# Last eight modulation chunks moved from the first feed-forward stage into the latent inverse, with columns by transposes and one fill copy placed earlier

## What is computed

```
mod   = silu(c)     @ w_mod + b_mod          # w_mod: 1024 x 6144, fp32, 24 MB
mod_c = silu(c_ctx) @ w_mod + b_mod
sh1, sc1, g1, sh2, sc2, g2 = split(mod, 6)   # shifts, scales and gates, 1024 values each
h  = rmsnorm(x) * norm1_g * (1 + sc1) + sh1            # latent
hc = rmsnorm(ctx) * norm1_g * (1 + csc1) + csh1        # context
... delta rule on hc, then on h; each needs the inverse of a unit lower triangular matrix per head and chunk
x = x + g1 * mix
x = x + g2 * swiglu(rmsnorm(x) * norm2_g * (1 + sc2) + sh2)
```

## Time and profile before

| | us |
|---|---|
| median of 3 runs (lowest, highest) | 1394.09 (1393.87, 1400.3) |
| the profiled execution's own time | 1391.02 |
| its span in the trace | 1389.0 |
| busy: PE / DVE / ACT / POOL | 1302.8 / 819.8 / 641.0 / 124.6 |

### The profile page before, as it was taken

How to read it: one execution, slowest core, us unless ns; L and a number is a source line. 1 busy time by engine, 2 the same in 40 slices (tenths; PEclk the granted TensorE clock), 3 DMA queues, 4 the chain that set the end, 5 groups by cost and what they waited for, 6 DMA issues and landing times.

```text
span 1389.0 us, 22276 instructions
## 1 busy us (share of the span) xinstructions
PE 1302.8 (94%) x9222; PEld 1189.4 (86%) x9222; DVE 819.8 (59%) x1189; ACT 641.0 (46%) x950; POOL 124.6 (9%) x108
## 2 busy tenths in 40 slices
PE   7987999999999999789999989988889999999997
PEld 6964988888898889679999988988789998899996
DVE  6672464544685756676655586576644566654444
ACT  6353353443556635434444356454136453544443
POOL 0130000000002112140001030023310000000000
PEclk9997999999999999999999999999999999999999
DMA  9558467776554344234443444542004555355540
GB/s 320 164 189 267 141 221 242 242 245 227 178 181 152 92 138 136 91 122 152 152 152 123 159 145 122 152 122 92 30 1 135 183 173 179 130 189 190 190 151 31
DMA packets 163802, 218.74 MB, mean 157 GB/s; under 512 B 5016, under 2 KB 134902, under 8 KB 163574
## 3 DMA queue, kind: packets, MB, share of 16 engines
q1 hardware_dynamic: 161842, 215.15, 47.5%
q10 hardware_dynamic: 1860, 2.16, 0.5%
HBM read 216.26 MB, written 1.05 MB: 156 GB/s over the span
## 4 chain that ended last, share of the span: by engine, by line
PE 64%; issue 20%; DVE 6%; ACT 2%; POOL 2%; DMA 2%; DVEq 2%; POOLq 2%; ACTq 0%; SPq 0%
PE bank L539 17%; PE bank L540 17%; PE bank L541 17%; PE bank L602 2%; DVE w_lo L530 1%; PE bank L1317 1%; DMA w_raw<-in_w_mod 1%; PE bank L1295 1%; PE bank L1524 1%; PE bank L824 1%; PE bank L1377 1%; PE bank L812 1%; PE bank L1302 1%; DVEq L2171 1%; DMA arena<-in_vec_rows 1%
## 5 line engine op out<-in xcount | busy, mean ns | idle before, releaser
L530 DVE TENSOR_TENSOR w_lo<-w_raw,w_hi 128x1024 fp32r<-128x1024 f32 (+1 forms) x350 | 423.4, 1250 | 167.8 <-ACT w_hi L521 161.5
L539 PE MATMUL bank<-act_hi,w_hi 128*128 128x256 f32 x1744 | 505.0, 290 | 18.2 <-DVE act_lo L2139 5.1
L540 PE MATMUL bank<-act_lo,w_hi 128*128 128x256 f32 x1744 | 498.5, 286 | 0.0
L541 PE MATMUL bank<-act_hi,w_lo 128*128 128x256 f32 x1744 | 498.1, 286 | 0.0
L521 ACT ACTIVATE w_hi<-w_raw 128x1024 fp32r<-128x1024 f32 (+1 forms) x350 | 348.9, 1041 | 102.8 <-PE bank L541 89.9
L539 PEld LDWEIGHTS bank<-act_hi,w_hi 128*128 128x128 f32 x1744 | 339.7, 195 | 33.7 <-issue 19.4
L540 PEld LDWEIGHTS bank<-act_lo,w_hi 128*128 128x128 f32 x1744 | 339.9, 195 | 1.0 <-issue 0.5
L541 PEld LDWEIGHTS bank<-act_hi,w_lo 128*128 128x128 f32 x1744 | 339.5, 195 | 0.0
L539 PE MATMUL bank<-w_hi,side_hi 128*128 128x512 f32 (+1 forms) x392 | 151.1, 386 | 0.0
L540 PE MATMUL bank<-w_lo,side_hi 128*128 128x512 f32 (+1 forms) x392 | 148.6, 379 | 0.0
L541 PE MATMUL bank<-w_hi,side_lo 128*128 128x512 f32 (+1 forms) x392 | 148.4, 379 | 0.0
(11 more groups left out here) (323 smaller groups left out, 1540.8 us busy)
## 6 DMA issues: line engine op xcount, KB each, us to landing
w_raw<-in_w_in SPq DMA_DIRECT2D x40, 1024.0 KB, 5.8
w_raw<-in_w_up SPq DMA_DIRECT2D x32, 1024.0 KB, 6.4
w_raw<-in_w_down SPq DMA_DIRECT2D x32, 1024.0 KB, 5.0
w_raw<-in_w_mod SPq DMA_DIRECT2D x24, 1024.0 KB, 5.3
w_raw<-in_w_ffn_in SPq DMA_DIRECT2D x22, 1024.0 KB, 5.2
w_raw<-in_w_gate SPq DMA_DIRECT2D x20, 1024.0 KB, 5.3
w_raw<-in_w_ffn_out SPq DMA_DIRECT2D x11, 1024.0 KB, 5.3
w_raw<-in_w_out SPq DMA_DIRECT2D x8, 1024.0 KB, 8.0
```

The lines of the kernel that those rows point to most:

```text
L530: nc.vector.tensor_tensor(wlo[:, slot, 0:n], raw[:, st.slot(name), n * half:n * (half + 1)], whi[:, slot, 0:n].bitcast(F32), ALU.subtract) ...
L539: nc.tensor.matmul(o, ahi, bhi, start=start, stop=False, skip_group_check=True)
L540: nc.tensor.matmul(o, ahi, blo, start=False, stop=False, skip_group_check=True)
L541: return nc.tensor.matmul(o, alo, bhi, start=False, stop=stop, skip_group_check=True)
```

## The change

1. `LATE_MODS = 8`: only pairs 6 and 7 stay in layer 0's feed-forward. Chunks 16 to 23 (pairs 8 to 11) are put in the stream behind the chunk `("post", 16)`, the first one of the branch merge, and are multiplied in the latent delta at points of the inverse.
2. The columns of every pair (also of 0 to 7) are made by four transposes of 128x128 against the identity; DVE sums the four strips with a reduce out of PSUM and adds the bias in a second instruction. The matrix `mod_sum` is gone.
3. `final_g` is computed with pair 3 (not with the last pair), the gains of the second norm with pair 9.
4. `settle()`: ACT copies `sc3`'s bank right before it copies the turned k and v, ahead of the chunk loop, and not at T0.
5. The rows of pairs 8 to 11 are copied into two scratch tiles of the delta (`scr[0]`, `scr[1]`).

```diff
+LATE_MODS = 8
-        ... ("pad", 1), ("mod_sum", 2),
+        ... ("pad", 1),
-    put("mod_sum", p % 32 == np.arange(2)[None, :])
+LAT_EXTRA = {"P": [("mod", 16), ("mod", 17), ("modr", 8)], "x0": [("modc", 8), ("mod", 18), ("mod", 19), ("modr", 9)],
+             "x1": [("modc", 9)], "z2": [("mod", 20)], "x2": [("mod", 21), ("modr", 10)], "t2": [("modc", 10)],
+             "z3": [("mod", 22)], "x3": [("mod", 23), ("modr", 11)], "t3": [("modc", 11)]}
+LAST_FILL = 6 + len(LAT_FILL)
-def filler(part, step):
+def filler(part, step, between=None):
...
     def fill(point, most=None):
+        for entry in LAT_EXTRA.get(point, []) if between else []:
+            between(*entry)
-for j in range(6, MOD_PAIRS):
+for j in range(6, LATE_MODS):
     for at, entry in ((0, ("mod", 2 * j)), (2, ("mod", 2 * j + 1)), (3, ("modr", j)), (4, ("modc", j))):
         FFN_EXTRA[0].setdefault(16 + 4 * (j - 6) + at, []).append(entry)
+LAT_MODS = mod(*range(2 * LATE_MODS, 2 * MOD_PAIRS))
...
         for l, src in enumerate(post_src):
             st.add(("post", l), src)
+            if l == LAST_FILL:
+                add_direct(LAT_MODS)
...
             act.drain().then_inc(S("dn_ecol"), 1)
+            if settle:
+                settle()
             for n in range(TT):
...
+        def rows_of(j):
+            return mod_rows[j % 4] if j < LATE_MODS else scr[j % 2]
...
                 for i in range(4):
-                    mm = nc.tensor.matmul(ps[b][:, 2 * i:2 * i + 2], mod_rows[j % 4][:, P * i:P * (i + 1)],
-                                          col("mod_sum", 0, 2), start=True, stop=True)
+                    mm = tr(ps[b][:, P * i:P * (i + 1)], rows_of(j)[:, P * i:P * (i + 1)])
...
+            def lat_mod(kind, x):          # PE; ACT's takes "modr", DVE's takes "modc"
+                if kind == "mod":
+                    mod_chunk(x, take)
+                elif kind == "modc":
+                    mod_columns(x)
...
-                if i:
+                if i and i - 1 not in settled:
                     lat_copy(i - 1)
+            def settle():
+                lat_copy(left[0] - 1)
+                settled.append(left[0] - 1)
...
-                free(v.tensor_tensor(modc[:, 4 * j:4 * j + 4, :], ps[b][:, 0:8].rearrange("p (m j) -> p m j", j=2),
-                                     bm, ALU.add), b)
+                parts = ps[b][:, :].rearrange("p (m k j) -> p m j k", m=4, k=4)[:, :, 0:2, :]
+                free(v.tensor_reduce(modc[:, 4 * j:4 * j + 4, :], parts, AX.X, ALU.add), b)
+                dve.drain()
+                v.tensor_tensor(modc[:, 4 * j:4 * j + 4, :], modc[:, 4 * j:4 * j + 4, :], bm, ALU.add)
...
-                if j == MOD_PAIRS - 1:
+                if j == 9:
                     dve.drain()
                     gain_of(2, "norm2_g_2", 32, 0)
+                if j == 3:
                     fn = vec[:, V["final_norm"]:V["final_norm"] + KT]
                     ...                    # final_g, as before
```

More of the change, by code:

```diff
@@ L70, in const_columns @@
     for name, width in (
-        ("ident", P), ("ones", P), ("rot", P), ("eps", 1), ("ln_q", 1), ("eps2", 1), ("even", 1), ("inv_freq", 1), ("pad", 1), ("mod_sum", 2),
+        ("ident", P), ("ones", P), ("rot", P), ("eps", 1), ("ln_q", 1), ("eps2", 1), ("even", 1), ("inv_freq", 1), ("pad", 1),
         ("mask", 3 * 384), ("inv_cnt", 2 * T),
@@ L908, in act_lat_inputs, with act_delta @@
             ln_exp_tables()
-        def act_delta(act, part, d_, fill):
+        def act_delta(act, part, d_, fill, settle=None):
             lat = part == "lat"
@@ L1545, in lat_fill @@
                 project(pe, ("post", n_tiles + i), lambda m: (b, T * m), KT, all_hi, all_lo)
+            def lat_mod(kind, x):
[3 more added lines that the diff above has]
+                    mod_columns(x)
             pe_lat_inputs(pe, take)
-            pe_delta(pe, "lat", D_LAT, take, filler("lat", lat_fill))
+            pe_delta(pe, "lat", D_LAT, take, filler("lat", lat_fill, lat_mod))
             l = n_tiles + len(LAT_FILL)
@@ L1633, in mod_copy @@
                 act.wait_ge(direct_done, st.direct["mod", 2 * j + 1] + 1)
-                nc.scalar.activation(mod_rows[j % 4], ps[banks.bank(f"mod{j}")][:, :], ACT.Copy).then_inc(S("mod_copied"), 1)
+                nc.scalar.activation(rows_of(j), ps[banks.bank(f"mod{j}")][:, :], ACT.Copy).then_inc(S("mod_copied"), 1)
             def rms(b, n, scale, out, power=-0.5, bias=eps_col):
@@ L1944, in lat_copy, with lat_mod @@
                     free(nc.scalar.activation(z_n[:, two, :], pair(b), ACT.Copy), b)
+            def lat_mod(kind, x):
+                if kind == "modr":
+                    mod_copy(x)
+            def settle():
+                lat_copy(left[0] - 1)
+                settled.append(left[0] - 1)
+            settled = []
             act_lat_inputs(act)
-            act_delta(act, "lat", D_LAT, filler("lat", lat_fill))
+            act_delta(act, "lat", D_LAT, filler("lat", lat_fill, lat_mod), settle)
             l = n_tiles + len(LAT_FILL)
@@ L2406, in lat_fill, with lat_mod @@
                         dve.drain().then_inc(S("sc_p"), 1)
+            def lat_mod(kind, x):
+                if kind == "modc":
+                    mod_sum(x)
             dve_lat_inputs(dve)
-            dve_delta(dve, "lat", D_LAT, filler("lat", lat_fill))
+            dve_delta(dve, "lat", D_LAT, filler("lat", lat_fill, lat_mod))
             l = n_tiles + len(LAT_FILL)
```

## The result

The changed kernel takes 1384.64 us in the median of 6 runs (1378.28 to 1387.75) beside 1393.98 us of the kernel before (1393.22 to 1400.3): 9.3 us less by the medians, ratio 0.9918 with a 95% interval of 0.9897 to 0.9939, which is 11.4 us (8.5 to 14.4). The prediction was 1386.0 us, a gain of 8.0.

A forecast was written before the change was run, and what follows sets the result against it. PE, busy 94% of the span, was taken to bound the kernel, with the latent delta a chain; -12.0 - 0.7 - 0.2 - 0.5 + 5.4 = -8.0 us from the 1394.09 us median gave 1386 us, range 1379.5 to 1391.5.

The forecast's parts named there:

- feed-forward, chunks and columns of pairs 6 to 11: Layer 0's feed-forward: removing eight chunks and four column sets saves 12.0 us of PE, transposed columns 0.7 us.
- attention part: Before layer 0's output projection: longer DVE sums cost 0.6 us, shorter columns bring chunk 11 forward 0.8 us; together -0.2.
- settle, to the second pair: Chunk loop of the latent delta: the early copy ends PE's T0 wait, so the second pair comes 6.4 us earlier.
- level 1's xz, what remains of it: Latent inverse: of the 6.4 us won by the early copy, 0.5 remain at level 1's xz.
- levels: Inside the inverse's levels: four chunks cost 4.4 us; with columns, bank and DVE sums +5.4 us.
- Where the loads go: Latent inverse, 937 to 1007 us: memory moves 30 and 1 GB/s, so nobody loads there.
- The list of signs: Marks expected in the later profile, such as 11.30 us step pairs and a wait of about 4 us before level 1.
- Chunk 19: Between X0 and level 1: its load, issued at 964.4, arrives at 969.8; PE waits from about 965.5, then clocks low.
- case A: Before level 1: no wait for chunk 19's load, xz starts 6.7 us earlier, sum -14.2 or 1379.9 us; chance 0.12.
- The bank of pair 9: Level 2's second z claims this bank, freed only after DVE's reduce behind its last subtraction: +0.25 us.
- Rival C: Levels of the inverse: the clock stays low, +2.8 us a level, sum +7.4 or 1401.5 us; chance 0.05.
- Rival B: Chunk loop: the early copy frees nothing, chunk 19 arrives at 976.2, sum -1.6 or 1392.5 us; chance 0.10.

The follow-up runs named there:

- second set: The changed kernel, unchanged, measured once more beside its variants: 1386.02 us against 1394.43 us, ratio 0.9945.
- b_settle: The kernel before with only the early copy of sc3's bank added: 1388.71 us against 1392.87 us, ratio 0.9960.
- a_early: The changed kernel with chunk 16 loaded ahead of ("post", 16) and multiplied at T3's fill: 1381.42 us against the kernel before's 1392.87 us, ratio 0.9915.
- a_empty: The changed kernel without the last eight modulation chunks, their 16 columns set to 0: 1374.08 us against the kernel before's 1392.87 us, ratio 0.9864.
- a_no_settle: The changed kernel without the early copy of sc3's bank: 1392.63 us against the kernel before's 1394.43 us, ratio 0.9984.

## Why the prediction was right, point by point

The mechanism was right in the main, and the sum to about 1 us; that it is so close is partly luck, since two of its terms failed in opposite directions. The forecast of -8.0 lies within the second set's interval (4.6 to 10.7 us less) and just outside the first's (8.5 to 14.4). By stages, each against the profile of before; the row of `settle` is contained in the one below it and not added again, and both measured sums take the average of stage a:

| term | predicted | measured |
|---|---|---|
| feed-forward, chunks and columns of pairs 6 to 11 | -12.7 | -13.5 (stage b) |
| attention part | -0.2 (-1.5 to +1.5) | +1.6 on average (stage a) |
| settle, to the second pair | -6.4 | -6.7 (stage d) |
| level 1's xz, what remains of it | -0.5 (-1.5 to +0.5) | -1.9 and -0.7 |
| levels | +5.4 (+3.5 to +8) | +5.2 (stage f) |
| sum | -8.0 | -8.6 and -7.4; medians -9.3 and -8.4 |

Where the loads go: the prediction read the two slices from 937 to 1007 us as 30 and 1 GB/s. They are 92 and 30; the 1 GB/s is the slice from 1007 to 1042. The idle stretch was thus less idle than said; no term of the sum rests on it.

Feed-forward: mis-sized by 0.8 us. I took 11.30 us for a step pair without chunks from the only one in the trace of before, directly behind the last columns. In the changed kernel the pair at that place also takes 11.29, and the later ones 11.22 on average. Eight pairs times 0.08 us is 0.6 of the 0.8.

Attention: this step failed. The wait at the output projection grew by 0.98 us (2.89 against 1.91), where the prediction said 0.6 for DVE's last stretch (its own terms, 0.3 + 0.6 + 0.3 - 0.49, give 0.7), and the 0.8 us that the shorter columns were to bring ahead of chunk 11 never showed: PE still waits 7.0 to 7.4 us for it in the kernels with transposes, and 6.6 to 7.1 in the four with products. The rest of the 1.6 us I can't give to the change: b_settle, with the old columns, has 50.89 us in stage a. The averages are 49.1 us over the four profiles with products and 50.7 over the eight with transposes.

Settle: right in mechanism and in size, and shown by both of its runs, adding it to the kernel before and taking it from the changed one. The list of signs puts the second pair 6.4 us behind the start of T0's projection; that is the shift, the distance worked out above it was 5.83 us, and 5.83 is what came.

Chunk 19: the step as I put it. It is issued behind the split of ("post", 16), PE stands 4.07 and 4.38 us for it (4.3 worked out), the clock is low behind it, and most of what settle won is lost there. The load took 5.15 and 5.47 us against the 5.37 that I used. The -1.9 us of the first profile is outside the bounds of -1.5 to +0.5, the -0.7 of the second inside: the z products behind the same kind of wait took 2.61 and 3.51 us, as the clock came back sooner or later. a_early showed the cause by taking the wait away; it also showed that case A, 6.2 us below the forecast, was too large by 0.7 to 1.9 us.

Levels: right within 0.3 us. From xz to xz it is 7.96, 8.20 and 7.30 us, then 6.11 and 6.06, where 6.06 is a level without chunks. The bank of pair 9 costs 0.37 us (a wait of 0.86 where others have 0.49), 0.25 was worked out. The first holds chunk 20 and the columns of pair 9 (+1.9), the second two chunks (+2.1), the third chunk 23 alone (+1.2). I had forecast 2.0 to 2.5 for levels 2 and 3 and nothing for 4: the sum holds, the marks were one chunk off.

Rival C did not come: from level 2 on the clock is 1.00 in every profile, with eight transposes a level, also where levels 1 to 3 have four more. In level 1 it can still be low (a_empty: 0.57 for the first 3 us from xz on). Rival B did not come either, but a_no_settle shows what it would have been: 7.8 to 9.1 us, not 6.4, since chunk 19's load then takes 6.95 us.

## What to carry to other kernels

In a ring of four slots a load is as late as the consumer of the chunk four places ahead of it in the list lets it be: before work with its own loads is moved into an idle stretch, list which slot each load takes and when that is freed, and see whether one of the new loads can go ahead of the last old one (worth 4.3 and 5.5 us here). Work put between the products of a serial chain costs its full length here, although the engine pauses several times in it; at the end of the chain the same four chunks, with the columns of their two pairs, cost 2.7 us instead of 4.3. And where runs of one kernel spread by 10 us, compare stages that repeat to hundredths, not spans.

## What the runs showed of the hardware

The granted clock also falls in stretches in which PE never stood: 0.66 from 512 to 522 us of the changed kernel with PE busy for all 10.00 us, in code that is the same before and ran at 1.00 there. It falls at about 514 us; just ahead of it PE makes 32 products of 128x16 (from 511.10), as it does in the kernel before (from 520.04), where the clock stays. In both kernels PE pauses there only for 0.20 us, shortly before these products. Over the twelve profiles layer 1 varies by 6.9 us, the slowest with a mean clock of 0.96 and the fastest with 0.98. What brings it about stays open. The Trainium skill (TensorE: Matmul & The Clock Gate, Part 1) has idle time lower the clock and activity release it; in this stretch the trace doesn't agree, as PE was busy ahead of it and in it.

DVE's small addition of eight columns took 1.11 us beside a busy POOL and 0.17 us without it:

```profile
959.30 1.11 DVE L2127 TENSOR_TENSOR mod_cols<-mod_cols,vec_cols 128x8 f32<-128x8 f32 x1
...
971.94 0.17 DVE L2127 TENSOR_TENSOR mod_cols<-mod_cols,vec_cols 128x8 f32<-128x8 f32 x1
```

```profile
957.90 2.49 POOL L1217 TENSOR_TENSOR arena<-arena 128x512 f32<-128x512 f32 x2 [0.32 <-issue]
```

POOL's two instructions end at 960.39, DVE's addition at 960.41; at 971.94 POOL has been idle since 971.24. DVE's splits show the same, also with two inputs in SBUF: the two halves of ("post", 16) take 3.50 us at 952.92, beside POOL's work from 952.01 on, where those of the chunk before, at 945.34, with POOL idle, take 2.36. The Trainium skill (SBUF — State Buffer, Who interferes with whom) says that a DVE instruction with two inputs in SBUF contends with a GpSimd instruction that reads SBUF, over a shared pair of ports that it calls an exclusive lock. The rows agree: the addition of 0.17 us has both inputs in SBUF, POOL's instructions read `arena`, and the addition ends with them, and the reduce 0.3 us ahead of it, which reads a bank, takes 0.19 us in both places. No run here took POOL's work away, so the cause isn't shown, only that the two come together.
